# A hybrid retention/RWKV/PEER block: the expert matrix U transposed in 32x32 blocks on VectorE instead of on TensorE

## What is computed

```python
h2 = rms_norm(x, norm2_w)
q = (h2 @ w_q).reshape(ntok, 8, 2, 128)
s1, s2 = q[:, :, 0] @ keys_1.T, q[:, :, 1] @ keys_2.T
v1, i1 = top_k(s1, 16); v2, i2 = top_k(s2, 16)
top, idx = top_k(v1[..., :, None] + v2[..., None, :], 16)
experts = i1[idx // 16] * 128 + i2[idx % 16]
gates = softmax(top)
act = gelu(einsum('nhkd,nd->nhk', expert_u[experts], h2)) * gates
out = einsum('nhk,nhkd->nd', act, expert_v[experts])
```

## Time and profile before

| | |
|---|---|
| median of 3 executions | 3006.19 us (3004.94 to 3009.53) |
| profiled execution, its span | 3002.4 us |
| PE busy | 2877.2 us (96%) |
| DVE busy | 1766.8 us (59%) |
| ACT busy | 1246.0 us (41%) |
| U stage, first to last transpose | 1206.8 to 2216.7 us |
| mean rate of the loads | 143 GB/s |

### The profile page before, as it was taken

One profiled execution on the slowest core, in us unless ns is written; L12 is line 12 of the kernel. 1 busy time (PEld: TensorE's weight loads), 2 busy tenths in 40 slices (PEclk: granted clock), 3 DMA queues, 4 the chain that ended last, 5 costly groups with the idle time before them and its releaser, 6 DMA issues.

```text
span 3002.4 us, 60128 instructions
## 1 busy us (share of the span) xinstructions
PE 2877.2 (96%) x21162; PEld 2727.8 (91%) x21162; DVE 1766.8 (59%) x3377; ACT 1246.0 (41%) x2261; POOL 146.0 (5%) x100
## 2 busy tenths in 40 slices
PE   7999969899999979999999999999999999999997
PEld 7999968888999979999999999999998888888886
DVE  4477863335646554895333333477778887666665
ACT  5446412224444544334433333322234444555554
POOL 0021043340000000000000000000000000000000
PEclk9999989999999999999999999999999999999998
DMA  6655610004655546444444444433335444666665
GB/s 184 182 167 154 185 42 1 1 0 127 183 168 175 176 149 203 127 139 139 140 140 140 140 140 140 134 117 112 112 120 161 154 160 156 194 193 193 194 192 187
DMA packets 222202, 429.21 MB, mean 143 GB/s; under 512 B 12965, under 2 KB 154663, under 8 KB 220455
## 3 DMA queue, kind: packets, MB, share of 16 engines
q1 hardware_dynamic: 222119, 428.07, 45.6%
HBM read 423.82 MB, written 4.19 MB: 143 GB/s over the span
## 4 chain that ended last, share of the span: by engine, by line
PE 91%; DVE 5%; issue 2%; ACT 1%; POOL 1%; DMA 0%; SPq 0%; DVEq 0%; ACTq 0%; POOLq 0%
PE PS L325 16%; PE PS L327 16%; PE PS L326 16%; PE PS L673 8%; PE PS L675 8%; PE PS L674 8%; PE PS L602 7%; PE PS L627 4%; PE PS L488 1%; PE PS L452 1%; PE PS L486 1%; PE PS L477 1%; DVE w_lo L1382 1%; DVE w_lo L1011 1%; PE PS L500 0%
## 5 line engine op out<-in xcount | busy, mean ns | idle before, releaser
L325 PE MATMUL PS<-act_hi,w_hi 128*128 128x256 f32 x4256 | 1231.0, 289 | 19.9 <-DVE w_lo L1011 18.9
L327 PE MATMUL PS<-act_hi,w_lo 128*128 128x256 f32 x4256 | 1207.0, 284 | 0.0
L326 PE MATMUL PS<-act_lo,w_hi 128*128 128x256 f32 x4256 | 1206.7, 284 | 0.0
L1011 DVE TENSOR_TENSOR w_lo<-raw,w_hi 128x512 fp32r<-128x512 f32 x1064 | 726.7, 703 | 303.8 <-ACT w_hi L709 300.0
L325 PEld LDWEIGHTS PS<-act_hi,w_hi 128*128 128x128 f32 x4256 | 818.7, 192 | 24.3 <-issue 15.5
L326 PEld LDWEIGHTS PS<-act_lo,w_hi 128*128 128x128 f32 x4256 | 819.5, 193 | 1.0 <-issue 1.0
L327 PEld LDWEIGHTS PS<-act_hi,w_lo 128*128 128x128 f32 x4256 | 818.6, 192 | 0.0
L709 ACT ACTIVATE w_hi<-raw 128x512 fp32r<-128x512 f32 x1064 | 637.5, 624 | 417.4 <-PE PS L327 416.6
L1382 DVE TENSOR_TENSOR w_lo<-PS,w_hi 128x512 fp32r<-128x512 f32 x512 | 335.6, 687 | 414.4 <-ACT w_hi L885 413.3
L885 ACT ACTIVATE w_hi<-PS 128x512 fp32r<-128x512 f32 x512 | 278.1, 596 | 368.9 <-PE PS L602 366.7
L673 PE MATMUL PS<-w_hi,act_hi 128*128 128x512 f32 x1024 | 404.8, 395 | 2.5 <-DVE w_lo L1011 2.5
(11 more groups left out here) (230 smaller groups left out, 1822.5 us busy)
## 6 DMA issues: line engine op xcount, KB each, us to landing
raw<-in_peer_u SPq DMA_DIRECT2D x256, 512.0 KB, 3.7
raw<-in_peer_v SPq DMA_DIRECT2D x256, 512.0 KB, 4.5
raw<-in_w_in SPq DMA_DIRECT2D x180, 512.0 KB, 3.8
raw<-in_w_out SPq DMA_DIRECT2D x32, 512.0 KB, 3.4
raw<-in_peer_w_q SPq DMA_DIRECT2D x32, 512.0 KB, 3.5
raw<-in_w_ret_branch SPq DMA_DIRECT2D x16, 512.0 KB, 3.4
raw<-in_w_rwkv_branch SPq DMA_DIRECT2D x16, 512.0 KB, 3.5
big<-in_x SPq DMA_DIRECT2D x2, 1024.0 KB, 6.2
```

Of the source, the lines that this page charges most:

```text
L325: pe.matmul(out, wh, xh, start=start, stop=False)
L326: pe.matmul(out, wh, xl, start=False, stop=False)
L327: return pe.matmul(out, wl, xh, start=False, stop=stop)
L1011: dve.tensor_tensor(w_lo[:, slot % 2, cols], raw[:, slot, cols], w_hi[:, slot % 2, cols].bitcast(f32), ALU.subtract).then_inc(S["unit_spli ...
```

## The change

1. `peer_u` is loaded a block (two units, 1 MB) at a time, in four DMAs. Each fills a quarter of the partitions with a quarter of the channels: partition 32q + i, position s holds channels 512q to 512q + 511 of expert 32s + i. A block lies in two neighbouring slots of `raw`.
2. In place of `ut`, DVE transposes all 32x32 blocks of half of a loaded block in place, in one instruction on 128 x 1024 elements (`u_turn`). Afterwards partition 32q + j holds, for each c, channel 512q + 32c + j of all 128 experts. So chunk c of the product has other channels than before. `norm2_w`, the rows of `peer_w_q` and the second norm's output are brought into the same order; `peer_w_q` is loaded by partition quarters too, 4 DMAs to a unit.
3. ACT and DVE make the high and low parts from `raw` instead of PSUM. A slot is free when `unit_split` has counted its unit.
4. DVE's order in unit k is: transpose of k, lo of k-1, then steps of the picks or of the gates. Each pick step is smaller (about half), and the picks have 30 instead of 13 iterations.
5. `iota` is copied to free places in PSUM, first in bank 0, later in bank 5, and the one-hots read it there. Buffers in `big` move.

```diff
-EXP_AT, PICKED_AT, GATE_AT = 13, 16, 48
+EXP_AT, PICKED_AT, GATE_AT = 30, 32, 48
...
+        iota_ps = [PS[:, 0, 0:P], PS[:, 5, 0:P]]
...
+        def u_raw(b):
+            return raw[:, 2 * b:2 * b + 2, :].rearrange("p a n -> p (a n)").rearrange("p (s d) -> p s d", s=4)
+        def u_part(k, at, n):
+            return u_raw(k // 2)[:, :, at * 32:(at + n) * 32].rearrange("p s (c j) -> p c s j", j=32)
...
+                        if name == "wq":
+                            wp = weight.rearrange("(q c j) n -> q j c n", q=4, j=32)
+                            for q in range(4):
+                                sp.dma_start(raw[32 * q:32 * q + 32, slot, :].rearrange("p (c n) -> p c n", c=4),
+                                             wp[q, :, 4 * kq:4 * kq + 4, ds(g * 256 + col0, 256)]).then_inc(S[f"raw_in{slot}"], 16)
...
-            u_rows = a["peer_u"][0].rearrange("(b e) n -> b e n", e=P)
+            u_rows = a["peer_u"][0].rearrange("(b s i) (q d) -> b q i s d", s=4, i=32, q=4)
...
-            def load_experts(rows, it, sem, value):
-                for k in range(4):
-                    sp.wait_ge(S[sem], value(k))
-                    sp.dma_start(raw[:, k, :], rows[ds(it * 2 + k // 2, 1), :, (k % 2) * 1024:(k % 2 + 1) * 1024]
-                                 .rearrange("a e n -> e (a n)")).then_inc(S[f"raw_in{k}"], 16)
-            load_experts(u_rows, 0, "unit_split", lambda k: 2 * (U0 + k) - 6)
+            def load_u(it, b):
+                for q in range(4):
+                    sp.dma_start(u_raw(b)[32 * q:32 * q + 32],
+                                 u_rows[ds(it * 2 + b, 1), q].rearrange("a i s d -> i (a s) d")).then_inc(S[f"raw_in{2 * b}"], 16)
+            for b in range(2):
+                sp.wait_ge(S["unit_split"], 2 * (U0 + 2 * b + 1) - 6)
+                load_u(0, b)
             with sp.Fori(1, BLOCKS // 2) as it:
-                load_experts(u_rows, it, "uT_bank", lambda k: it * 8 + 2 * k - 6)
+                for b in range(2):
+                    sp.wait_ge(S["unit_split"], it * 8 + (2 * U0 + 4 * b - 4))
+                    load_u(it, b)
...
-                            sp.wait_ge(S["uT_bank"], 4 * BLOCKS + 2 * k - 6)
+                            sp.wait_ge(S["unit_split"], 2 * V0 - 4 + 4 * (k // 2))
...
-            def ut(it, k):
-                pe.wait_ge(S[f"raw_in{k}"], it * 16 + 16 * (U0 // 4 + 1))
-                for hh in range(2):
-                    pe.wait_ge(S["unit_split"], it * 8 + (2 * (U0 + k) - 3 + hh))
-                    for c in range(4):
-                        last = pe.transpose(PS[:, 2 * (k % 2) + hh, c * P:(c + 1) * P],
-                                            raw[:, k, (4 * hh + c) * P:(4 * hh + c + 1) * P], ident)
-                    last.then_inc(S["uT_bank"], 1)
...
-                    if k < 3:
-                        ut(it, k + 1)
-                    elif not final:
-                        ut(it + 1, 0)
                     um(it, k)
...
-                    act.wait_ge(S["uT_bank"], it * 8 + (2 * k + hh + 1))
+                    act.wait_ge(S["uT"], it * 4 + (k + 1))
                     act.wait_ge(S["half_used"], it * 8 + (2 * (U0 + k) - 3 + hh))
-                    act.activation(w_hi[:, k % 2, hh * 512:(hh + 1) * 512], PS[:, 2 * (k % 2) + hh, :], ACT.Copy).then_inc(S["unit_hi"], 1)
+                    act.activation(w_hi[:, k % 2, hh * 512:(hh + 1) * 512].rearrange("p (c s i) -> p c s i", c=4, s=4),
+                                   u_part(k, 4 * (2 * (k % 2) + hh), 4), ACT.Copy).then_inc(S["unit_hi"], 1)
...
-            def u_lo(it, k, between=iter(())):
+            def u_lo(it, k):
                 for hh in range(2):
                     dve.wait_ge(S["unit_hi"], it * 8 + (2 * (U0 + k) + hh + 1))
                     cols = slice(hh * 512, (hh + 1) * 512)
-                    dve.tensor_tensor(w_lo[:, k % 2, cols], PS[:, 2 * (k % 2) + hh, :], w_hi[:, k % 2, cols].bitcast(f32),
+                    dve.tensor_tensor(w_lo[:, k % 2, cols].rearrange("p (c s i) -> p c s i", c=4, s=4),
+                                      u_part(k, 4 * (2 * (k % 2) + hh), 4),
+                                      w_hi[:, k % 2, cols].bitcast(f32).rearrange("p (c s i) -> p c s i", c=4, s=4),
                                       ALU.subtract).then_inc(S["unit_split"], 1)
-                    next(between, None)
+            def u_turn(it, k, between=iter(())):
+                if k % 2 == 0:
+                    dve.wait_ge(S[f"raw_in{k}"], it * 64 + (LANDED["u"] + 64))
+                turned = u_part(k, 8 * (k % 2), 8)
+                dve.transpose(turned, turned).then_inc(S["uT"], 1)
+                if k > 0:
+                    u_lo(it, k - 1)
+                elif not (isinstance(it, int) and it == 0):
+                    u_lo(it - 1, 3)
+                next(between, None)
+                next(between, None)
...
-                dve.tensor_tensor(hotB[par], bc(iota, 4), bc(eg[:, 1, ds(i * (4 * GATE_STEPS[part]) + 4 * k, 4)], P, 2), ALU.is_equal)
+                dve.tensor_tensor(hotB[par], bc(iota_ps[part], 4), bc(eg[:, 1, ds(i * (4 * GATE_STEPS[part]) + 4 * k, 4)], P, 2), ALU.is_equal)
                 yield
                 for t in range(4):
-                    last = dve.tensor_scalar(hotA[:, 4 * par + t, 0:hi_ - lo_], iota[:, lo_:hi_], eg[:, 0, ds(i * (4 * GATE_STEPS[part]) + (4 * k + t), 1)],
+                    last = dve.tensor_scalar(hotA[:, 4 * par + t, 0:hi_ - lo_], iota_ps[part][:, lo_:hi_], eg[:, 0, ds(i * (4 * GATE_STEPS[part]) + (4 * k + t), 1)],
...
-                    u_lo(it, k, gate_step(i, k, 0))
+                    u_turn(it, k, gate_step(i, k, 0))
...
+            u_lo(BLOCKS // 2 - 1, 3)
             gate_in(15, 3, 0)
+            dve.wait_ge(S["gelu1"], BLOCKS // 2)
+            link(dve.tensor_copy(iota_ps[1], iota))
```

More of the change, by code:

```diff
@@ L184, in hybrid_block_kernel @@
         St = [d["S"].rearrange("p (n c) -> p n c", n=2) for d in place]
-        keysT = flat(Z(49, 50))
-        SC = [flat(Z(50 + 8 * t, 58 + 8 * t)).rearrange("p (j k) -> p j k", k=P) for t in range(2)]
+        keysT = flat(Z(73, 74))
+        SC = [flat(Z(74 + 8 * t, 82 + 8 * t)).rearrange("p (j k) -> p j k", k=P) for t in range(2)]
         eg = extra[:, 0:768].rearrange("p (w n) -> p w n", w=3)
@@ L645, in _ @@
             pe.wait_ge(S["picked"], 2)
-            for w, src in enumerate((66, 68, 70)):
+            for w, src in enumerate((90, 92, 94)):
                 for tt in range(2):
@@ L701, in _, with hi @@
             ch = Chain(act, S["act_chain"])
-            def hi(m, slot, hh, first=False):
+            def hi(m, slot, hh, first=False, stage=None):
                 if hh == 0:
-                    act.wait_ge(S[f"raw_in{slot}"], m * 16 + 16)
+                    if stage == "wq":
+                        act.wait_ge(S[f"raw_in{slot}"], m * 64 + (LANDED["wq"] + 64 - 64 * (SEG["wq"][0] // 4)))
+                    elif stage == "v":
+                        act.wait_ge(S[f"raw_in{slot}"], m * 16 + (LANDED[f"v{slot % 2}"] + 16 - 16 * (V0 // 4)))
+                    else:
+                        act.wait_ge(S[f"raw_in{slot}"], m * 16 + 16)
                 if not first:
@@ L721, in body @@
                         for hh in range(2):
-                            hi(m, slot, hh, first)
+                            hi(m, slot, hh, first, name)
                         if kq == 1 and evac and not (isinstance(g, int) and g == 0):
@@ L918, in v_hi @@
                         for hh in range(2):
-                            hi(it + (V0 + h * BLOCKS) // 4, k, hh)
+                            hi(it + (V0 + h * BLOCKS) // 4, k, hh, stage="v")
                 if h == 0:
@@ L1337, in pick_steps @@
                     v16, i16, i16f, top, tix = places(tt)
-                    tmp_i = [big[:, 80 + tt, w * P:(w + 1) * P].bitcast(u32) for w in range(2)]
-                    tmp_f = [big[:, 82 + tt, w * P:(w + 1) * P] for w in range(2)]
+                    tmp_i = [big[:, 104 + tt, w * P:(w + 1) * P].bitcast(u32) for w in range(2)]
+                    tmp_f = [big[:, 106 + tt, w * P:(w + 1) * P] for w in range(2)]
                     dve.wait_ge(S["sc_copied"], tt + 1)
@@ L1342, in pick_steps @@
                     link(dve.tensor_copy(i16f, i16))
[L1343 removed]
+                    cand = flat(Z(108, 116)).rearrange("p (h i j) -> p h i j", h=8, i=16)
                     vv = v16.rearrange("p (h w) k -> p h w k", w=2)
[L1345 to L1347 removed]
+                    for e in range(0, 8, 4):
+                        link(dve.tensor_tensor(cand[:, e:e + 4], vv[:, e:e + 4, 0, :].unsqueeze(3).broadcast_to([P, 4, 16, 16]),
+                                               vv[:, e:e + 4, 1, :].unsqueeze(2).broadcast_to([P, 4, 16, 16]), ALU.add))
+                        yield
                     yield from top16(cand.rearrange("p h i j -> p h (i j)"), 8, top, tix)
@@ L1417, in gate_turn @@
                         dve.wait_ge(S["gelu1"], GATE_AT)
```

(6 more changed lines are left out.)

72 lines of the change are left out of this document (40 added, 32 removed).

## The result

The changed kernel takes **3399.82 us** (median of 4 executions, 3394.34 to 3408.95) against 3005.57 of the kernel before beside it: a ratio of 1.132, 95% interval 1.130 to 1.134. It is slower by 394 us, where 290 were forecast. The median lies on the upper edge of the range, and the ratio applied to the time the prediction started from, 3006.19, gives 3403, just outside. The direction and both waits were right, the price of each was too small. The profiled execution has a span of 3392.5 us, 390.1 more than before.

What follows compares the result with a forecast made beforehand. PE was taken to bound the U stage, its 223 us saving lost to new waits: +174 us for serial loads, +115 for the gating loop, +1 at the stage's end, total +290 on 3006.2, so 3296 us; range 3130 to 3400.

Steps and rivals of the forecast that it cites:

- both waits: U stage: blocks without gating wait for serial loads, +174 us; gating units wait in a serial loop, +115 us.
- One load at a time: Ungated U blocks: DVE's order lets only one load be under way, 9.30 us a block against 7.48, +174 us.
- The cover of the picks: Ungated U blocks: DVE's work with the top-16 picks, 6.9 us a block, hides below the load-bound 9.3.
- the four issues hide in it: `peer_u` block load: SP's four issues at 0.33 us, the fourth 1.0 us after the first, add nothing to 6.5.
- The gating loop: Gating units of the U stage: DVE and PE wait for each other serially, 6.4 us against 4.61, +115 us.
- 24 products 2.87: Term of the gating unit: PE's 24 products take 2.87 us of the 6.4.
- the lower clock: Rival, U stage: PE at half speed throughout, blocks 11.5 us, gating units 10.1, about 3745 us; chance 0.03.
- The row I took for safety: Profile row on PE's clock: a stretch with 3.28 busy of 5 us still has a granted clock of 1.00.
- full-rate quarters: Rival, `peer_u` loads: four quarters flow like a whole load, 5.0 us, a block 7.80, 3153 us; chance 0.22.
- slow transposes: Rival, DVE in the U stage: a transpose takes 2.29 us instead of 1.22, 3467 us; chance 0.08.
- gating not serial: Rival, gating units: DVE's own 4.6 us sets the unit, 0 instead of +115, 3181 us; chance 0.06.
- faster: Rival, U stage: loads so quick that PE sets the pace, 2955 us; chance 0.04.

Runs made afterwards that it cites:

- e4: The change with the last lo of a block moved ahead of the next block's first transpose in DVE's order: 3071.91 us.
- e6: e1 with one 1 MB DMA per block over all partitions, in runs of 8 KB, instead of four DMAs: 3190.81 us.
- e1: The change with each of a block's four loads filling all 128 partitions and a quarter of the columns (U's order wrong): 3260.1 us.
- e2: The change with 16 idle transposes on TensorE ahead of each gating unit's wait for lo: 3340.55 us.
- e8: The change with loads and releases by the unit and the gate multiplication put off by one more unit: 2895.64 us, 0.964 of the kernel before.
- e10: e8 with the comparisons reading the iota table from SBUF again instead of its copy in PSUM: 2882.22 us.
- e3: The change with the gate multiplication put off by one more unit (that of unit k-2 in unit k): 3240.85 us.
- e9: The change with idle transposes on TensorE in every unit of the stage, 12 without gating and 16 with it: 3339.43 us.

## Why the prediction came out as it did

**One load at a time: right.** The chain of the changed kernel runs through first transpose, two lo's, issue, load, in this order, and moving one lo (e4) took 270 us from the ungated part. The cover of the picks was right too: with more than one load under way (e4) they set the pace while they run, at about 7.1 us a block against the prediction's 6.9.

**The load: the term that was too small.** Forecast 6.5, measured 7.1; the block 9.7 on average (932 / 96) against 9.30, 38 us in all, since the handover and the transpose with its two lo's together took 0.2 less than their terms. The step that failed is "the four issues hide in it", a term of nothing. Forecast were 5.0 for a whole load, 1.5 for the span and 0 for the four pieces; e6, e1 and the change (4.9, 5.8 and 7.1) give 4.9, 1.3 and 0.9. The issues came 0.50 us apart, not 0.33: 0.32 for the issue itself and the rest register work, so the fourth went out 1.5 us after the first. How much of the 0.9 is this and how much the shorter runs stays open. The price of the span was about right: in the middle of a load the changed kernel shows 238 GB/s at a DMA share of 0.98, as the earlier trace rows had 234 at 1.04:

```profile
1804.50:1807.50 3.00, 3.00 (x21) 3.00 (x21) 0.18 (x1) 0.85 (x2) 0.00 (x0) 0.73 0.98 238
```

The Trainium skill ("SBUF — State Buffer", Door 1: The DMA port swizzle, and the section behind it, "Can I just issue two DMAs to hit both halves?") puts the ceiling for 32 or 64 partitions at some 218 GB/s and says that DMAs to the two halves serialize. The trace agrees on the direction, e1 being the test, and has 238 over these 3 us, above that figure. The estimate of 6.9 us by the page was nearer to the measured 7.1 than mine, but by luck: it has 1.9 for the span, where e1 shows 1.3, and like mine nothing for the four pieces.

**The transpose: right.** 1.24 us against 1.22, with the bounds of 0.69 and 2.29 both far. The Trainium skill ("Vector Engine (DVE) Microarchitecture Reference", 3.8) has one element per cycle per lane, an estimated 1.07 us; the next instruction starts 1.17 after the transpose, 0.1 more, so the trace agrees roughly.

**The gating loop: the wait was right, its products were priced at one clock.** At full clock the unit takes 6.47 (e2) against the forecast 6.4, and the part 122 us more than before against 116. But in the change the unit averaged 7.4 (474 / 64), and e2 shows that the other 55 us are the clock. The step that failed is the term "24 products 2.87" at a clock of 1.00 in every unit, with the lower clock as a rival of 0.03 and one price, half speed throughout, 3745 us. The runs showed in its place a clock that falls after some of the gaps, for part of a unit (about half of the units take 7.8 to 9.2 us), and that costs 55 us, only where PE is in the loop. The row I took for safety, 3.28 busy of 5 us at 1.00, was one short stretch. With the block at its measured 9.7 and this case at its 55 us, the sum would have been 3296 + 38 + 55 = 3389; the profiled execution took 3394.

**The rest.** `peer_w_q` by quarters was free. The one-hots from PSUM stand ahead of DVE's wait in the change, so they were free there, as said; they cost 11 us once DVE had become the bound (e8 to e10). The rivals of full-rate quarters, slow transposes, gating not serial and faster are excluded by e1, by the transpose's row, by e3 and by the result, in this order.

## What to carry to other kernels

When a step moves from a producer's buffer to a shared one, ask which instruction now frees the buffer and what stands ahead of it in its engine's queue: here one subtraction behind a transpose let only one load run at a time and turned a saving of 0.87 us a unit into a loss. A wait that was harmless because the engine waited for already had its next unit becomes a loop when that unit stands behind the wait; follow it around once. And where the bound moves off TensorE, price its products at both levels of the clock wherever a wait on both sides makes them part of the loop; here the truth lay between the two.

## What the runs showed of the hardware

- In the change PE idled 2.2 to 2.5 us ahead of its products, and the granted clock fell to 0.51 for 3 us in the middle of some of them; after another gap of the same 2.46 us it stayed at 1.00. With idle transposes in all these gaps (e9) it was 1.00 in both parts. The 1024 transposes of e2 made the kernel 59 us faster (3399.8 to 3340.6).
- In such a stretch three products took 0.64 us from start to start instead of 0.36, a factor of 1.8.
- The same 1 MB took 4.9 us in one DMA (e6), 5.8 in four over all partitions (e1) and 7.1 in four of 32 partitions each (the change). SP issued one DMA each 0.50 us.
- VectorE's transpose of 128x1024 float32 in 32x32 blocks takes 1.24 us, as long as two subtractions of 128x512 (1.25).
